# Squares of the attention output moved from ScalarE to VectorE, x loaded before the last heads, and a new order of GpSimd, ScalarE and VectorE work at the entry of the up projection

## What is computed

```python
o_fox = fox_attention(...)                      # softmax with forget sums, 8 heads of 64
o_sb = stick_breaking_attention(...)            # sigmoid and a running product, 8 heads
o = jnp.concatenate([rmsnorm_2(merge_heads(o_fox), fox_out_g[l]),
                     rmsnorm_2(merge_heads(o_sb), sb_out_g[l])], axis=-1)
x = x + o @ w_out[l]
h = rmsnorm_2(x, ffn_norm_g[l])
u = causal_dwconv(h @ w_up[l], conv_w[l], conv_b[l])
```

## Time and profile before

| | us |
|---|---|
| median of 3 runs | 2567.57 |
| the profiled execution's own time | 2568.96 |
| its span | 2567.2 |
| around the span | 1.8 |

### The profile page before, as it was taken

The page is one execution under the profiler, slowest core; times in us unless marked ns, Lnnn a source line. Parts: engine busy times, 40 slices in busy tenths (PEclk is TensorE's granted clock), DMA queues, the critical chain, the costliest instruction groups (busy, mean ns, idle before and its releaser), DMA issues. The chain is left out here.

```text
span 2567.2 us, 31717 instructions
## 1 busy us (share of the span) xinstructions
PE 2507.9 (98%) x12610; PEld 2091.0 (81%) x12610; DVE 1509.7 (59%) x1462; ACT 1029.1 (40%) x1528; POOL 1060.3 (41%) x617
## 2 busy tenths in 40 slices
PE   8999999999999999999999999999989999999999
PEld 4888788888888888888788888887867888887887
DVE  5864557665666753444545546464987677675324
ACT  3421043435344331023456655565344444442214
POOL 3765453333434335542121121203567877762320
PEclk9999999999999999999999999999999999999999
DMA  8222231212212144242111011013212222235311
GB/s 343 82 89 72 95 96 52 69 58 66 71 66 78 50 179 149 97 138 78 42 42 42 34 34 41 34 50 132 91 58 99 74 83 91 74 122 218 127 41 66
DMA packets 66238, 226.07 MB, mean 88 GB/s; under 512 B 7816, under 2 KB 11784, under 8 KB 64816
## 3 DMA queue, kind: packets, MB, share of 16 engines
q1 hardware_dynamic: 49824, 169.00, 18.6%
q10 hardware_dynamic: 16272, 55.09, 6.0%
HBM read 174.22 MB, written 45.65 MB: 86 GB/s over the span
## 5 line engine op out<-in xcount | busy, mean ns | idle before, releaser
L264 POOL TENSOR_TENSOR w_hi<-w_raw,ones 128x1024 fp32r<-128x1024 f32 x67 | 178.7, 2667 | 528.9 <-PE G L238 471.8
L269 POOL TENSOR_TENSOR w_lo<-w_raw,w_hi 128x1024 fp32r<-128x1024 f32 x88 | 237.8, 2702 | 181.4 <-ACT w_hi L263 176.3
L238 PE MATMUL G<-H_hi,w_hi 128*128 128x512 f32 x928 | 290.2, 394 | 1.0 <-ACT silu_zB L724 0.7
L238 PE MATMUL G<-H_lo,w_hi 128*128 128x512 f32 x928 | 285.9, 389 | 0.0
L238 PE MATMUL G<-H_hi,w_lo 128*128 128x512 f32 x928 | 285.8, 389 | 0.0
L238 PEld LDWEIGHTS G<-H_lo,w_hi 128*128 128x128 f32 x928 | 174.2, 188 | 36.5
L238 PEld LDWEIGHTS G<-H_hi,w_lo 128*128 128x128 f32 x928 | 174.2, 188 | 36.4
L238 PEld LDWEIGHTS G<-H_hi,w_hi 128*128 128x128 f32 x928 | 171.6, 188 | 36.9 <-issue 3.7
L1989 POOL TENSOR_TENSOR w_lo<-w_raw,w_hi 128x1024 fp32r<-128x1024 f32 x24 | 60.1, 2506 | 319.7 <-ACT w_hi L2236 319.7
L2110 PEld LDWEIGHTS G<-att_v,probsT 128*128 128x128 f32 x1152 | 147.2, 193 | 23.4 <-ACT probsT L2265 14.3
L2052 PE MATMUL G<-A_hi,w_hi 128*128 128x512 f32 x368 | 152.3, 414 | 8.9 <-DVE projected L2472 8.3
(11 more groups left out here) (602 smaller groups left out, 6271.0 us busy)
## 6 DMA issues: line engine op xcount, KB each, us to landing
w_raw<-w_in SPq DMA_DIRECT2D x65, 512.0 KB, 3.3
up_raw<-w_up SPq DMA_DIRECT2D x44, 512.0 KB, 4.9
pre_raw<-w_in SPq DMA_DIRECT2D x30, 512.0 KB, 3.3
act_d<-made SPq DMA_DIRECT2D x22, 512.0 KB, 2.9
wm<-w_mod SPq DMA_DIRECT2D x8, 1024.0 KB, 18.2
w_raw<-w_out SPq DMA_DIRECT2D x16, 512.0 KB, 3.3
x_d<-x ACTq DMA_DIRECT2D x16, 512.0 KB, 2.9
x<-x_d SPq DMA_DIRECT2D x16, 512.0 KB, 9.3
```

The lines of the kernel that those rows point to most:

```text
L238: mm = nc.tensor.matmul(dst[:, n * NB:n * NB + c], w[:, k, :], m[:, k, n * NB:n * NB + c], start=first, stop=last)
L264: eng.tensor_tensor(dst, src, ones.unsqueeze(1).to_broadcast([P, kt, P]), ALU.mult)
L269: nc.gpsimd.tensor_tensor(w_lo[:, slot, 0:kt, :], w_raw[:, slot, 0:kt, :], w_hi[:, slot, 0:kt, :].bitcast(F32), ALU.subtract).then_inc(w_r ...
```

## The change

1. In all rounds but the last, ScalarE's eight squares become three VectorE operations in the next round: `round_squares` (128x512, ON times ON) behind `chain` at m = 1 and at m = 2, and `round_sums` (a reduction of 128x1024 to 128x8) at m = 7. The last round's squares stay on ScalarE.
2. The copy-out of the first projection half of round 1 (q = 1, h = 0) moves one step up, ahead of `chain(1)`.
3. SyncE loads heads 4, 5, 6, then all of x, then heads 7, 0, 1, 2.
4. At the entry of the up projection: the sum for the seventh tile (k = 5) moves behind `sums_low(2)`, and the square of the last tile (k = 7) behind ScalarE's `sums_high(2)`; GpSimd makes S1 and S2 of pair 1 only after `sums_low(2)`, instead of ahead of S3 of pair 0; ScalarE's copy of product 11 of pair 2 moves ahead of `tap(1, 0)`.

```diff
+            load_heads(HEAD_TILES[:3])
             S.wait(sp, "pe", "values", ROUND_GROUPS * (ROUNDS - 1) - 1)
             for k in range(KT):
                 sp.dma_start(X2[:, k, :], x2_d[k]).then_inc(x2_landed, 16)
+            load_heads(HEAD_TILES[3:])
...
-                        squares(r - 1, m - 2)
...
+            def round_squares(r, part):
+                if r == 0:
+                    v.wait_ge(nf_stored, 16)
+                me("round sums", r - 1)
+                dst, src = squared[:, 4 * part:4 * part + 4, :], ON[:, 4 * part:4 * part + 4, :]
+                do("round squares", v.tensor_tensor(dst, src, src, ALU.mult), 2 * r + part)
+
+            def round_sums(r):
+                for part in range(2):
+                    me("round squares", 2 * r + part)
+                do("round sums", v.tensor_reduce(ssp[:, r, :], squared, AX.X, ALU.add), r)
...
-                if q < ROUNDS and n in EVAC_AT[q % 2]:
-                    evac(q, EVAC_AT[q % 2][n])
+                for at, h in EVAC_AT[q % 2].items():
+                    if q < ROUNDS and n == at - (q == 1 and h == 0):
+                        evac(q, h)
...
                     chain(s + 1)
+                r, m = divmod(s, TILES)
+                if 1 <= r < ROUNDS and m in (1, 2):
+                    round_squares(r - 1, m - 1)
+                if 1 <= r < ROUNDS and m == 7:
+                    round_sums(r - 1)
...
             low(0, "S1")
-            first_made(1)
             made_sum(0, "S3", raw_part(0, "11"), raw_part(0, "21"), ALU.subtract)
             low(1, "11")
             low(0, "S3")
             low(0, "22")
+            S.wait(g_, "dve", "sums' low part 2 3")
+            first_made(1)
...
             sums_high(2, slice(3, 4))
+            squared_tile(KT - 1)
             slabs_high(1, UP_ORDER[1:])
...
+            first_copied(2)
             tap(1, 0)
             slabs_high(2, UP_ORDER[5:])
-            first_copied(2)
...
-            for i in (2, 3):
-                for js in parts_of:
-                    sums_low(i, js)
+            for js in parts_of:
+                sums_low(2, js)
+            S.wait(v, "act", "out2 square", KT - 3)
+            me("out2 sum", KT - 5)
+            do("out2 sum", v.tensor_tensor(S2, S2, bs[:, 1, :], ALU.add), KT - 3)
+            for js in parts_of:
+                sums_low(3, js)
```

More of the change, by code:

```diff
@@ L1748, in program @@
         dump = take("squares_made", [P, P])
+        squared = fwork.rearrange("p (t d) -> p t d", d=P)
         rs = take("row_sums", [P, TILES])
@@ L2282, in probs, with last_squares @@
                 S.mark("act", "made", act.activation(p, p, ACT.Exp, scale=-1.0, bias=mn[:, g % 2, :], accum_out=rs[:, n:n + 1]), g)
[L2284 to L2289, removed]
+            def last_squares():
+                S.wait(act, "dve", "out", STEPS // 4 - 1)
+                for t in range(TT):
+                    if t:
+                        S.wait(act, "act", "square", t - 1)
+                    S.mark("act", "square", act.activation(dump, ON[:, t, :], ACT.Square, accum_out=ssp[:, ROUNDS - 1, t:t + 1]), t)
             def outT(r):
@@ L2341, in _ @@
                         act.dma_start(fsum[1], nf_d[r:r + 1, :].to_broadcast([P, T])).then_inc(nf_landed[1], 16)
[L2342 to L2347, removed]
-                        squares(r - 1, m - 2)
-            for part in range(2):
-                squares(ROUNDS - 1, part)
+                    if r and m == 2:
+                        outT(r - 1)
+                        for half in range(2):
+                            S.wait(act, "act", "outT", 2 * r - 2 + half)
+                        act.dma_start(o_d[out_row(r - 1)], OT).then_inc(o_stored[out_row(r - 1)], 16)
+            last_squares()
             S.wait(act, "pe", "sb spread")
@@ L2401, in _ @@
                     S.mark("act", "first product", act.activation(first_product, G[1][:, 0:NB], ACT.Copy), 0)
-                if i:
-                    S.wait(act, "dve", "out2 sum", OUT_ORDER[i - 1])
-                S.mark("act", "out2 square", act.activation(bs[:, 1, :], X2[:, k, :], ACT.Square), k)
+                if i < 7:
+                    squared_tile(i)
                 if i < 7:
@@ L2519, in out_of @@
                     S.wait(v, "pe", "out turned", 2 * r - 1)
-                    S.wait(v, "act", "square", TT * r - 1)
+                    for part in range(2):
+                        me("round squares", 2 * r - 2 + part)
                 dst, src = ON[:, t0:t0 + 4, own_rows(hh)], V[:, 0:4 * HD].rearrange("p (b d) -> p b d", d=HD)
@@ L2560, in _ @@
                 if s == STEPS - 2:
-                    S.wait(v, "act", "square", TT * (ROUNDS - 1) - 1)
+                    me("round sums", ROUNDS - 2)
                     do("sb squares", v.tensor_reduce(ss[:, 0, :], ssp.rearrange("p (i x) t -> p x t i", x=2)[:, 0], AX.X, ALU.add))
@@ L2568, in _ @@
             out_of(STEPS // 4 - 1)
-            S.wait(v, "act", "square", TT * ROUNDS - 1)
+            S.wait(v, "act", "square", TT - 1)
             do("fox squares", v.tensor_reduce(ss[:, 1, :], ssp.rearrange("p (i x) t -> p x t i", x=2)[:, 1], AX.X, ALU.add))
@@ L2631, in _ @@
                     second_sums(i - 5)
[L2632 to L2635, removed]
+                if i < KT - 2:
+                    S.wait(v, "act", "out2 square", k)
+                    if i:
+                        me("out2 sum", OUT_ORDER[i - 1])
+                    do("out2 sum", v.tensor_tensor(S2, S2, bs[:, 1, :], ALU.add), k)
                 out2_low(k, read_of(k), "out2 lo", k)
```

13 lines of the change are left out of this document (10 added, 3 removed).

## The result

The changed kernel takes 2548.93 us, the median of four runs (2545.80 to 2549.88), against 2567.12 of the kernel before: ratio 0.9928, 95% interval 0.9916 to 0.9940, so 18.2 us faster. The profiled execution took 2548.83 us, with a span of 2547.0.

A forecast was written before the change was run, and what follows sets the result against it. TensorE, busy 98% of the span, bounds the kernel, so only its waits and low clock can be won. 4.3 + 8.7 + 4.9 + 2.8 = 20.7 off 2568.96 gives 2548.3 profiled, 2547 as median; range 2540 to 2557 us.

The forecast's parts named there:

- A: Round 0's start: earlier copy-out removes TensorE's 2.76 us wait and the low clock behind it; gain 4.3 us.
- B: Rounds 1 to 6: squares off ScalarE end TensorE's waits for copies, VectorE's additions covered by idle time; gain 8.7 us.
- C: Round 7: first half without squares takes 12.6 us, earlier x loads remove the wait for x; gain 4.9 us.
- D: Entry of the up projection: wait ahead of product 12 of pair 2 goes, earlier gains given back; gain 2.8 us.
- Rival (2): Only the entry of the up projection goes wrong, -2 us there: 2552 us; chance 0.15.
- (1): Attention: VectorE takes ScalarE's place, its products late in s rounds and blocked in round 7: 2554 us; chance 0.2.
- (3): Entry of the up projection: GpSimd in time, spread 3 us sooner, gain 6 us there: 2544 us; chance 0.15.
- (4): Attention: VectorE bounds every round, 52 us added against at most 25 won: 2595 us; chance 0.02.
- (5): Attention: copies really wait on exponentials, so only A and a little of C remain: about 2562 us; chance 0.05.

The follow-up runs named there:

- e1: Kernel before with only the copy-out of round 1's first projection half moved one step up: 2563.63 us, ratio 0.9989.
- e2: Kernel before with only the squares of rounds 1 to 6 moved to VectorE, x still loaded behind the heads: 2557.99 us, ratio 0.9964.
- e4: Kernel before with only the new order at the entry of the up projection: 2566.88 us, ratio 1.0000.
- e3: Kernel before with only x loaded ahead of the last four heads: 2565.67 us, ratio 0.9993.
- a8: Changed kernel with GpSimd's splits of heads 4 to 7 held until VectorE's last two squares are done: 2548.32 us, 0.9919 of the kernel before.
- a5: Changed kernel with GpSimd's S1 and S2 of pair 1 back ahead of S3 of pair 0: 2544.61 us, 0.9905 of the kernel before.
- a6: Changed kernel with ScalarE's root and copy of product 11 of pair 1 ahead of two high parts: 2546.77 us, 0.9916 of the kernel before.
- a9: Changed kernel with the reduction of round 6's squares at step 3 of round 7 instead of step 7: 2548.03 us, one run.
- a7_twice: Changed kernel with each of the 14 squares' products done twice: 2553.55 us, 0.9942 of the kernel before.
- b3: Changed kernel with a5's and a6's edits and GpSimd's split of head 7 held back: 2544.34 us, 0.9901 of the kernel before.
- b1: Changed kernel again, unaltered, on another chip: 2548.76 us, 0.9922 of the kernel before.

## Why the prediction was right, point by point

The median came 1.9 us above the predicted 2547, inside the range. In the profiled execution 20.1 us went where 20.7 were forecast. So close a total is partly luck: at the sites of the change 22.1 us went, and 2.0 were lost in unchanged code, at 50 us. The bounds of the parts add up to 6.3 to 27.5 us, not to the 8 to 27 of the prediction; nothing hangs on it.

- **A, 4.3 forecast; the wait right, the clock's share not certain.** 4.4 between the two profiles, 4.3 in e1. The scan ended when it had, no wait came in its place. But the 1.7 us of clock in it are no fixed price of the 2.76 us wait: they followed it in the profiles of before, e2 and e4 and not in e3, and against e3 the part is worth 2.8 us, the lower bound. The run times give 2.8 (0.5 to 5.1).
- **B, 8.7 forecast, right in kind, 1.6 too small.** The two profiles show 10.3 us, and so does e2 alone. TensorE's waits in these rounds fell from 6.2 to 0.2 us for ScalarE's copies, the 6.0 of the forecast, and from 4.8 to 2.6 for the copy-outs, 2.2 where I took 2.7. The missing 2.1 are in TensorE's busy time, 437.9 us before and 435.7 after. The clock is not the cause, it is 1.00 in all of rounds 1 to 6 in both. What follows is a reading of the timelines, not tested by itself: six matmuls in a row behind a wait take 0.88 us and twelve 1.55, so 0.11 each and some 0.2 us for starting, which a matmul that follows at once does not pay; nine waits fewer (7 to 1 and 9 to 6) make 2. The term that was too small is the price of a wait, which the list of waits alone does not carry. That VectorE's additions are covered was right: twice as many products changed rounds 0 to 6 by less than 0.1 us. The reduction, put at 1.4, takes 1.22.
- **C, 4.9 forecast, 4.9 in the first profile, and both partly luck.** The first half of round 7 was right: 12.4 us for 12.6, the products late as forecast, though a8 puts what GpSimd held up at 0.5 and not 1.1 us. The step that failed is the one on the second half: that head 7, coming later, is needed only at 1782. Its data is, but its split runs on GpSimd beside the scaling of x and costs TensorE 1.2 to 1.9 us of wait in five of six profiles (the changed kernel twice, a5, a6, a8, a9) and 1.7 us or more of low clock behind it: the second half of round 7 takes 20.8 to 24.6 us there and 18.0 in the first profile. It was offset by something I had also missed: the 0.77 us wait for x in the profile of before was short because the clock had slowed the first half; e1 and e4 show 4.50 and 3.32 at the same place. Over the profiles the old round 7 takes 46.0 us on average (before, e1, e4), the changed 42.0 (the changed kernel twice, a9, a5, a6): 4.0.
- **D, 2.8 forecast, 2.5 in the profile.** The mechanism went as described: the first gap 0.49 (0.8 forecast), S3 of pair 1 made 12.9 us behind the low sums (13.3), the spread waiting 3.93 (4), a fall of the clock with it, no wait ahead of 12 of pair 2. As a mean over profiles it is 2.4, for the entry; the run times of e4 (0, 2.3 either way) put it there or lower. Rival (2), nothing or less from this part, is not excluded by them.
- **The rivals.** (1), VectorE in ScalarE's place, is refuted for rounds 1 to 6 by a7_twice, and is true in kind of round 7, where two more products made the first half 5.2 us longer. (3) did not happen; (4) and (5) are refuted by e2.

What stays open: how much of D is real in the run times, and how much of a5's and b3's gain is fewer falls of the clock by their order of gaps, rather than by chance.

## What to carry over

Count in a profile what the clock took, stage by stage, before costing anything by it: here the one profile of the kernel before had an entry 1.3 us longer than the mean of four like it, and a wait for x 2.6 to 3.7 us shorter than two others, in unchanged code. Do the same to a gain: the low clock behind a wait is won only in those runs in which it would have fallen, as e3 shows for part A. When two loads are swapped, follow the later one past its landing, to the operation that it starts on an idle engine, and ask which engine shares that memory then. And an addition to an engine is cheap only where nobody blocks it: the same 0.69 us product was free in six rounds and took up to 2.75 us in the seventh and held up TensorE.

## What the runs showed of the hardware

- **The clock.** The granted clock falls for stretches that lose 1.7 or 3.4 us (0.83 or 0.66 over 10 us), 5.1 once (a8), at places that change from run to run with the same code: the unchanged entry took 75.4 to 79.8 us. The wait of 2.76 us in round 0 was followed by a fall in three profiles and not in e3. Behind a wait of 2.96 us at 1874.84 the clock stayed at 1.00 to 1890 in the first profile; behind one of 2.93 at the same place in b1 (1876.50) it was 0.78 in 1880 to 1890. Run times of the kernel before scatter from 2563.5 to 2574.7 us, while with the clock's part taken off their means agree within 0.8 us on three chips. I had written that a wait of over 2 us costs another 1.6 to 3.2: it may.
- **What blocks what.** A product of 128x512 with two inputs in SBUF took 0.69 us alone, 1.53 to 2.75 beside GpSimd operations of 2.4 us; a scaling of 128x1024 by a second tensor in SBUF and a column 1.28 alone and 2.65 to 3.34; a reduction of 128x1024 1.21 either way; GpSimd's own operations went from 2.37 to 2.8, and once to 3.24.
- **Without a fall of the clock a stage is exact.** In nine profiles with the changed attention rounds 0 to 6 took 485.4 to 485.6 us, with no fall of the clock in any. Against that, a difference of some tenths in a stage length means something, where a difference of 2 us in run times does not. It holds only as long as the clock does: with the old attention and the old copy-out before and e4 have 500.3 and 500.1 us and e3 498.7.
